# Latent keys' squares summed token by token among gate products, with small roots spread and turned

## The reference, cut to what matters

```
def rms_norm_2(x, g):
    xf = x.astype(jnp.float32)
    y = xf * lax.rsqrt(jnp.mean(xf * xf, axis=-1, keepdims=True) + EPS)
    return (y * g.astype(jnp.float32)).astype(x.dtype)

k_m = jnp.concatenate([k_nope, k_rope], axis=-1)      # [.., 8 heads, 64 + 32]
q_m = rms_norm_2(q_m, p['g_mla_q'])
k_m = rms_norm_2(k_m, p['g_mla_k'])
if rope_m is not None:                                # x only, not the context
    cos, sin = rope_m
    q_m = ...apply_axial_rope(q_m[..., MLA_NOPE:], cos, sin)
    k_m = ...apply_axial_rope(k_m[..., MLA_NOPE:], cos, sin)
```

## Time and profile before

| | us |
|---|---|
| median of three runs | 2583.94 |
| the profiled execution | 2575.13 |
| its span, first to last instruction | 2573.3 |
| TensorE busy | 2537.3 (99%) |
| VectorE busy | 2064.2 (80%) |
| ScalarE busy | 1292.7 (50%) |

### The profile page before, as it was taken

The page is one execution under the profiler, slowest core; times in us unless marked ns, Lnnn a source line. Parts: engine busy times, 40 slices in busy tenths (PEclk is TensorE's granted clock), DMA queues, the critical chain, the costliest instruction groups (busy, mean ns, idle before and its releaser), DMA issues.

```text
span 2573.3 us, 49828 instructions
## 1 busy us (share of the span) xinstructions
PE 2537.3 (99%) x20114; PEld 2360.8 (92%) x20114; DVE 2064.2 (80%) x3076; ACT 1292.7 (50%) x1778; POOL 52.5 (2%) x68
## 2 busy tenths in 40 slices
PE   8999999999999999999999999999999999999999
PEld 8998799999988899998889999885999988859999
DVE  7996589899876499957887876787887877978877
ACT  5345553353353453355665445546544465465543
POOL 0000000000011000000000000000000000000000
PEclk9999999999999999999999999999999999999999
DMA  7764267667632077753424554340355543404554
GB/s 293 286 237 168 95 236 287 230 269 277 220 115 99 18 272 261 261 181 144 151 99 165 181 190 184 134 162 15 134 198 190 184 149 146 164 1 148 196 181 145
DMA packets 61518, 454.60 MB, mean 177 GB/s; under 512 B 6872, under 2 KB 6896, under 8 KB 9280
## 3 DMA queue, kind: packets, MB, share of 16 engines
q1 hardware_dynamic: 54720, 394.24, 42.5%
q0 software_dynamic: 6656, 58.35, 5.8%
HBM read 451.49 MB, written 1.07 MB: 176 GB/s over the span
## 4 chain that ended last, share of the span: by engine, by line
PE 85%; DVE 10%; ACT 4%; issue 1%; DMA 0%; DVEq 0%; SPq 0%; ACTq 0%
PE ps L822 20%; PE ps L655 15%; PE ps L656 15%; PE ps L657 15%; PE ps L1116 3%; PE ps L1552 2%; DVE w_parts L2398 1%; PE ps L1411 1%; DVE half_parts L2603 1%; PE ps L1569 1%; PE ps L597 1%; PE ps L1586 1%; ACT half_parts L1846 1%; PE ps L1479 1%; PE ps L1423 1%
## 5 line engine op out<-in xcount | busy, mean ns | idle before, releaser
L1759 ACT ACTIVATE w_parts<-ring 128x1024 fp32r<-128x1024 f32 x462 | 463.1, 1052 | 347.7 <-PE ps L655 345.1
L655 PE MATMUL ps<-normed_parts,w_parts 128*128 128x256 f32 x2160 | 602.4, 279 | 1.7 <-DVE w_parts L2398 1.7
L656 PE MATMUL ps<-normed_parts,w_parts 128*128 128x256 f32 x2160 | 603.9, 280 | 0.0
L657 PE MATMUL ps<-normed_parts,w_parts 128*128 128x256 f32 x2160 | 603.3, 279 | 0.0
L2398 DVE SCALAR_TENSOR_TENSOR w_parts<-ring,w_parts 128x1024 fp32r<-128x1024 f32 x462 | 544.5, 1219 | 18.4 <-ACT w_parts L1759 17.4
L822 PE MATMUL ps<-stream_high,half_parts 128*128 128x256 f32 x2288 | 437.5, 287 | 3.2 <-DVE half_parts L2603 2.3
L655 PEld LDWEIGHTS ps<-normed_parts,w_parts 128*128 128x128 f32 x2160 | 406.0, 188 | 2.3 <-DVE w_parts L2398 2.3
L657 PEld LDWEIGHTS ps<-normed_parts,w_parts 128*128 128x128 f32 x2160 | 406.0, 188 | 0.0
L656 PEld LDWEIGHTS ps<-normed_parts,w_parts 128*128 128x128 f32 x2160 | 405.8, 188 | 0.0
L2603 DVE SCALAR_TENSOR_TENSOR half_parts<-ring,half_parts 128x1024 fp32r<-128x1024 f32 x233 | 281.5, 1214 | 117.5 <-ACT half_parts L1846 116.8
L822 PEld LDWEIGHTS ps<-stream_high,half_parts 128*128 128x128 f32 x2288 | 358.2, 188 | 9.5 <-issue 7.9
(11 more groups left out here) (504 smaller groups left out, 3826.5 us busy)
## 6 DMA issues: line engine op xcount, KB each, us to landing
ring<-in_weights SPq DMA_DIRECT2D x373, 1024.0 KB, 4.8
arena<-in_mod_weights POOLq DMA_DIRECT2D x32, 1536.0 KB, 6.7
arena<-in_cond POOLq DMA_DIRECT2D x8, 512.0 KB, 6.0
arena<-toeplitz_rows POOLq DMA_DIRECT2D x1, 1536.0 KB, 10.5
x<-in_x SPq DMA_DIRECT2D x1, 1024.0 KB, 4.8
arena<-in_ctx POOLq DMA_DIRECT2D x1, 1024.0 KB, 9.5
out<-x SPq DMA_DIRECT2D x4, 256.0 KB, 2.6
arena<-in_rope POOLq DMA_DIRECT2D x1, 640.0 KB, 11.7
```

The source lines that it names most:

```text
L655: first = pe.matmul(into, wh, high, start=start, stop=False, skip_group_check=True)
L656: pe.matmul(into, wh, low, start=False, stop=False, skip_group_check=True)
L657: return first, pe.matmul(into, wl, high, start=False, stop=stop, skip_group_check=True)
L1759: a(w_parts[:, to, 0, cols], ring[:, at, cols], ACT.Copy).then_inc(s["w_high"], 1)
```

## The change

Before, every partition held the sums of all keys (96x2048), and root and reciprocal ran on all 96 equal copies. After it, the sums are token-major. Sixteen products per stream, one for each head and half of the tokens, have 96x128 of the squares as stationary operand and a column of ones moving; they write one column each of a 128x16 tile in PSUM bank 4, and stand among the blocks of a gate pair. ScalarE takes the root of 128x16, VectorE inverts it and spreads it into a table (`root_table`, 128 x 2 x 8 x 96). Sixteen transposes (`latent_key_rows`) turn the table into 96x2048 in PSUM banks 4 to 7, from where the scaling of the keys reads it. The new semaphore `key_rows` is raised by VectorE when the table is ready and by TensorE when it is turned.

```
-        std_m = carve(6264, MH, S)
+        key_roots = carve(6264 + NT * MH * QK, MH * NT)
+        root_table = carve(6264, NT, MH, QK)
...
+            def latent_key_sums(at):
+                j, tt = at // NT, at % NT
+                mm = pe.matmul(ps[:, 4, at:at + 1], sq[0:QK, j, tt * P:(tt + 1) * P], C("ones", 1)[0:QK], start=True, stop=True)
+                if at == NT * MH - 1:
+                    mm.then_inc(s["mk_ss"], 1)
+
+            def latent_key_rows(t):
+                pe.wait_ge(s["key_rows"], 2 * t["i"] + 1)
+                for j in range(MH):
+                    for tt in range(NT):
+                        to = (j % 2) * S + tt * P
+                        mm = pe.transpose(ps[0:QK, 4 + j // 2, to:to + P], root_table[:, tt, j, :], C("ident"))
+                mm.then_inc(s["key_rows"], 1)
...  TensorE, opening of a stream
                 if i == 3:
-                    latent_key_sums(STREAMS[2])
+                    pe.wait_ge(s["mk_sq"], 3)
                 if full:
+                    split_one((0, 1), among=latent_key_sums if i == 3 else None)
                     split_one((0, 1))
-                    split_one((0, 1))
+                    if i == 3:
+                        latent_key_rows(STREAMS[2])
                     split_pairs(2)
...  TensorE, gates of a full stream
-                latent_key_sums(t)
-                gates_at()
+                pe.wait_ge(s["mk_sq"], i + 1)
+                split_one((0, 1), among=latent_key_sums)
+                split_pairs(1)
+                latent_key_rows(t)
                 if t["rope"]:
                     r = 2 * t["layer"]
-                    pe.wait_ge(s["mk_std"], i + 1)
+                    split_pairs(1)
+                    pe.wait_ge(s["mk_normed"], i + 1)
...                  (the keys' rotation now comes one pair behind rot_g, not two)
...  ScalarE
+                    high_halves(t, 28)
                 actv.wait_ge(s["in_normed"], 2 * i + 2)
                 actv.wait_ge(s["mk_ss"], i + 1)
-                root(std_flat, sums, QK).then_inc(s["mk_std"], 1)
+                root(key_roots, ps[:, 4, 0:MH * NT], QK).then_inc(s["mk_std"], 1)
...  VectorE
+                lows(*((t, 28) if full else (STREAMS[i + 1], 4)))
                 dve.wait_ge(s["mk_std"], i + 1)
+                link(nc.vector.reciprocal(key_roots, key_roots))
+                roots = key_roots.rearrange("p (j t) -> p t j", t=NT).unsqueeze(3).broadcast_to((P, NT, MH, QK))
+                nc.vector.tensor_copy(root_table, roots).then_inc(s["key_rows"], 1)
+                lows(*((t, 30) if full else (STREAMS[i + 1], 6)))
                 if full:
-                    link.mark(nc.vector.reciprocal(q_scale, q_scale))
+                    link(nc.vector.reciprocal(q_scale, q_scale))
+                dve.wait_ge(s["key_rows"], 2 * i + 2)
+                scale(kf, V("g_mla_k", l)[0:QK], ps[0:QK, 4:8, :].rearrange("p b (m t) -> p (b m) t", m=2)).then_inc(s["mk_normed"], 1)
                 if not t["rope"]:
-                    key_reciprocals(range(MH))
-                    scale_keys()
+                    lows(*((t, 34) if full else (STREAMS[i + 1], 12)))
...                  (in rotated streams lows(t, 32) stands where four reciprocals were)
```

More of the change, by code:

```diff
@@ L440, in build @@
             bonus_biased rw_turned rw_v_turned rwA rwA_copied rwA_masked rw_ab diag_kept small_done small_zero small_spread top_B top_Bs top_C top_T rw_x rw_xs rw_u rw_us rw_y rw_s rw_ys rw_ys2 rw_s0
-            gn_sum gn_mean gn_sq y_ready
+            gn_sum gn_mean gn_sq key_rows y_ready
             c_ready cond_in cond_ready mod_used mod_done w_high w_low h_high h_low half_high half_low half_used stream_h_high stream_h_low up_used conv_done silu_ready in_sq in_ss in_std in_normed glu_gated glu_in glu_sum glu_sq glu_ss glu_std glu_norm part_high part_low branch_sum
@@ L1415, in one @@
                 mm_n[0] += 1
[L1418 to L1425, removed]
+            left = {0: (s["x_ready"], 6 * QUARTERS), 1: (s["c_ready"], 2 * QUARTERS), 2: (s["x_ready"], 8 * QUARTERS), 3: (s["mk_normed"], 3)}
+            def latent_key_sums(at):
[10 more added lines that the diff above has]
+                mm.then_inc(s["key_rows"], 1)
             def stream(t):
@@ L1522, in stream @@
                     pe.matmul(ps[:, 6, 0:S], rot_g, k_g[:, slot:slot + S], start=True, stop=True).then_inc(s["rot_m_done"], 1)
-                    gates_at()
-                    pe.wait_ge(s["mk_normed"], i + 1)
+                    split_pairs(1)
                     pe.wait_ge(s["rot_used"], r + 2)
@@ L2275, in keep_last_gates @@
                     mm_n[0] += 1
-                std_flat, sums = std_m[0:QK].rearrange("p m t -> p (m t)"), ps[0:QK, 4:8, :].rearrange("p b t -> p (b t)")
                 if full:
@@ L3149, in stream @@
                         depthwise_conv((0, 1, 2), range(tap, tap + 1))
-                if not full:
-                    lows(STREAMS[i + 1], 4)
+                lows(*((t, 28) if full else (STREAMS[i + 1], 4)))
                 dve.wait_ge(s["mk_std"], i + 1)
[L3154 to L3164, removed]
+                link(nc.vector.reciprocal(key_roots, key_roots))
+                roots = key_roots.rearrange("p (j t) -> p t j", t=NT).unsqueeze(3).broadcast_to((P, NT, MH, QK))
+                nc.vector.tensor_copy(root_table, roots).then_inc(s["key_rows"], 1)
+                lows(*((t, 30) if full else (STREAMS[i + 1], 6)))
                 if full:
-                    link.mark(nc.vector.reciprocal(q_scale, q_scale))
+                    link(nc.vector.reciprocal(q_scale, q_scale))
+                dve.wait_ge(s["key_rows"], 2 * i + 2)
+                scale(kf, V("g_mla_k", l)[0:QK], ps[0:QK, 4:8, :].rearrange("p b (m t) -> p (b m) t", m=2)).then_inc(s["mk_normed"], 1)
                 if not t["rope"]:
-                    key_reciprocals(range(MH))
-                    scale_keys()
+                    lows(*((t, 34) if full else (STREAMS[i + 1], 12)))
                     if not full:
@@ L3178, in stream @@
                     fold = lambda v: v.rearrange("p b (m t) -> p (b m) t", m=2)
-                    key_reciprocals(range(4))
+                    lows(t, 32)
                     dve.wait_ge(s["rot_m_done"], 3 * l + 1)
                     tt(sq[0:QK], fold(ps[0:QK, 4:8, :]), over(sin_m, QK, MH), ALU.mult).then_inc(s["rot_used"], 1)
-                    key_reciprocals(range(4, MH))
-                    scale_keys()
                     lows(t, 35)
```

## The result

The changed kernel takes 2611.32 us (median of six runs, 2599.51 to 2630.95) against 2578.07 us (six runs, 2574.33 to 2584.39): ratio 1.0133, 95% interval 1.0101 to 1.0164. It is slower, as forecast, but by 33 us where 13.4 were forecast, and its runs spread over 31 us where those of before spread over 10. The time itself lies 13.9 us above the 2597.4 forecast; the change is 19.9 us dearer than forecast, and the two differ because the three runs on record before had a median of 2583.94, 5.9 us above that of the six. The profiled execution took 2612.23 us with a span of 2610.1, which is 36.8 more than before.

What follows compares the result with a forecast made beforehand. It took the tensor engine, busy 99% at full clock, as the bound. Tensor work +8.0, opening stalls +7.5 and old waits -2.1 gave +13.4 us on the earlier median of 2583.94: 2597.4 us, range 2587 to 2607.

Steps and rivals of the forecast that it cites:

- The tensor work: All four streams: one-column sums and transposes added, wide key sums removed, 4 x (3.70 + 1.75 - 3.44) = +8.0 us.
- one-column sums: Sixteen per stream among gate blocks, priced like the queries' at 0.231 us each: 3.70 us a stream, 14.8 in all.
- turns: Sixteen transposes per stream bringing the table into rows, at 0.109 us each: 1.75 us a stream, 7.0 in all.
- Setting its price aside: For the transposes, the trace's 0.109 us pitch was taken over the skill's 275 ns, which would cost some 10.5 us more.
- The two stalls of the opening: Stream 3's opening: tensor engine waits 3.7 us for the split behind the root, 3.8 behind the scaling; +7.5 us.
- The two old waits: Tensor engine's idle 0.92 us in stream 0 and 1.19 us in stream 3's opening should go: -2.1 us.
- Copy and scaling: Vector engine, per stream: copy to 128x1536 some 1.04 us; scaling of the keys stays at 2.34 us, reading PSUM.
- New waits, full streams ... No stall.: Streams 0, 1 and 3: half tiles in hand and the table's timing leave the tensor engine no new wait.
- the only passage with a clock in it: On transposes: the skill says they don't count as clock activity; the trace's clock stays full through 320 turns.
- a split behind the scaling in full streams too: Rival: each of three streams pays the scaling once, 6.9 us more, 2604.3 us; chance 0.10.

Runs made afterwards that it cites:

- e4: The changed kernel with half tile 25 split earlier in each full stream and the engines splitting further ahead in stream 3's opening; 2580.33 us, ratio 1.0018.
- e1: The changed kernel with half tile 25 of each full stream split earlier on ScalarE and VectorE; 2591.28 us, ratio 1.0068.
- e2: The kernel before with the wide key sums of each full stream one pair of gate blocks later, no one-column key sums or transposes; 2590.96 us, ratio 1.0067.
- e9: The kernel before with squares and ones of its wide key sums in the rounded 32-bit type, and half tile 25 split earlier; 2569.39 us, ratio 0.9975.
- e3: The changed kernel with ScalarE and VectorE splitting further ahead before they wait in stream 3's opening; 2606.51 us, ratio 1.0105.
- e7: The kernel before with wide key sums one pair later and 16 unread one-column products among the blocks behind each pause; 2614.87 us, ratio 1.0159.
- e5: The changed kernel with five useless products filling the tensor engine's pause ahead of the sums of each full stream; 2597.61 us, ratio 1.0090.

## Why the prediction was wrong

**Right by its own steps.** The tensor work: one-column sums at 0.58 us from block to block, turns 1.75 us for sixteen (1.75 forecast), and in e4, where nothing else is left, +5.3 us for +5.9. The Trainium skill says that a transpose takes about 275 ns in a kernel's context and doesn't count as activity (page "TensorE: Matmul & The Clock Gate", Part 4). Setting its price aside was right: 272 ns is the length of a record here, and 109 ns the pitch. Whether turns count as activity no run here shows; e4 has all 64 of them at full clock, so here they cost no clock. The two stalls of the opening: 3.60 and 3.66 us for 3.7 and 3.8, each released as described. The two old waits: both gone. Copy and scaling: 0.96 us for 1.04, 2.34 for 2.34.

**Wrong: "New waits, full streams ... No stall."** The step counted half tiles from the sums on, and there it holds. It did not ask what the removed instruction had hidden. The 3.44 us of the wide sums were booked as tensor time to be had, 3.44 out and 3.70 in; but the new sums lie among blocks that need the next half tile at once, while the old ones needed none and let a vector engine catch up that was 1.7 us behind. The term is 3 x 1.81 = +5.4 us. The row that says so was in the trace of before: the split that starts at 1210.48 and ends after the old sums have begun.

**Wrong by omission: the clock.** The sum had no term for it, since the clock was full throughout before, and the only passage with a clock in it was about the transposes. The runs show about 19 us in the profiled execution, most of it behind the 1.8 us pauses. It is the larger part of the error. In costs over the kernel before, the changed kernel less e1 is 17.0 us: 5.4 of pauses, and the other 11.6 is clock in the full streams. e1 less e4 is 11.0: 7.3 of waits (7.5 forecast) and 3.7 of clock. e4 itself is 5.3 (5.9 forecast). So the 19.9 us of error are 5.4 of waits and 15.3 of clock, less 0.8 by which the other terms were too high. The range, up to 2607, was set for a surprise in the size of instructions and had no room for a different state of the engine.

The rival "a split behind the scaling in full streams too" had 6.9 us for the 5.4 of the pauses, but in the wrong place: the turned rows cause no wait there. That its 2604.3 us lies nearer to the result is luck.

## What to carry to other kernels

Before you take an instruction out of a full engine, ask what ran behind it on the others: a block of work that needs no new input is where a late producer catches up, and its removal shows up as a wait, not as a gain (the changed kernel, e2 and e9 each show one, and e1 takes it away again). A pause of 2 us on the tensor engine may cost 8 more in clock if thin work comes next; split the next operands earlier, or put dense products, even useless ones, into the pause. And price a replacement by its distance from start to start: sixteen products of one column cost as much as four of 512.

## What the runs showed of the hardware that was not expected

The granted clock fell to 0.50 behind a pause of 1.8 us followed by a pair of blocks with one-column products between them, and stayed there for 17 to 20 us; it rose 2 to 5 us after the pair had ended in each of the five such falls (the changed kernel, e3, e7). Behind the same pause with plain blocks it fell for 3.4 us once and not at all twice (e2's profiled run). It is not certain from run to run: mean clocks of the changed kernel were 0.984 to 0.999. The kernel before also loses clock now and then: 3 of the 17 runs beside e1 to e4 had a mean clock of 0.996 and took 2582 to 2585 us, the other 14 were at 1.000 and at 2572.9 to 2578.1; beside e5, e7 and e9 it was 2 of 15. None of these was profiled; 0.004 of 2575 us is what one fall of 20 us to half clock, like the one in e3's attention, would take. Why the clock falls in one stream and not in the next was not settled.

A 96x512 product in the rounded type took 0.23 us from start to start (four in 0.93) against 0.86 in plain 32 bits.
